# Loading x ahead of the small vectors, and giving the context rows a root of their own

## The reference, cut to what matters

```python
mods_x = jnp.split((silu_c @ w_mod[l] + b_mod[l])[:, None, :], N_MOD, axis=-1)    # 2048 -> 6 * 2048
mods_c = jnp.split((silu_cc @ w_mod[l] + b_mod[l])[:, None, :], N_MOD, axis=-1)
nc = modulated_norm(h_c, attn_norm[l], mods_c[0], mods_c[1])   # rmsnorm(x) * g * (1 + scale) + shift
pc = nc @ w_in[l][:, Q_END:KR_END]                             # context: keys and values only
nx = modulated_norm(h_x, attn_norm[l], sa_x, sca_x)
... = jnp.split(nx @ w_in[l], ...)                             # latent: q, kv, rotary key, short convolution
o_mla = mla_attention(...)                                     # 8 heads, latent queries, latent + context keys
h_new = h_x + ga_x * merge_head_groups(o_mla, o_conv, p)
h_new = h_new + gf_x * moe_ffn(modulated_norm(...), p)         # router, 32 experts (top 4), shared expert
return rmsnorm(h_x, final_norm)
```

## Time and profile before

| | |
|---|---|
| median of 3 runs | 1144.02 us (1142.94 to 1144.53) |
| the profiled execution's own time | 1142.15 us |
| its span, first to last instruction | 1140.3 us |
| PE busy | 1024.8 us (90%) |
| DVE busy | 551.8 us (48%) |
| ACT busy | 223.3 us (20%) |
| loads and stores | 380.30 MB, mean 334 GB/s |
| chain that ended last | PE 70%, DMA 12%, DVE 8%, SP's queue 4%, ACT 4% |

### The profile page before, as it was taken

How to read it: one execution, slowest core, us unless ns; L and a number is a source line. 1 busy time by engine, 2 the same in 40 slices (tenths; PEclk the granted TensorE clock), 3 DMA queues, 4 the chain that set the end, 5 groups by cost and what they waited for, 6 DMA issues and landing times.

```text
span 1140.3 us, 15754 instructions
## 1 busy us (share of the span) xinstructions
PE 1024.8 (90%) x6029; PEld 575.9 (51%) x6041; DVE 551.8 (48%) x1104; ACT 223.3 (20%) x449; POOL 8.7 (1%) x13
## 2 busy tenths in 40 slices
PE   0899999999999998999989998987979988998985
PEld 0544578888875355444476753333334334333431
DVE  1300186854814783885465053454255354455433
ACT  4311110000002354010142022122022122123112
POOL 0000000000000000000000000000000000000002
PEclk9899999999999999999999999999989999999998
DMA  8989979999845736999709989999999999999994
GB/s 333 390 325 389 381 233 361 371 346 324 276 160 185 257 111 220 330 387 344 253 22 354 389 332 370 409 409 408 407 409 408 407 406 408 409 407 409 409 404 188
DMA packets 158359, 380.30 MB, mean 334 GB/s; under 512 B 10498, under 2 KB 44112, under 8 KB 157136
## 3 DMA queue, kind: packets, MB, share of 16 engines
q1 hardware_dynamic: 158288, 379.35, 88.9%
HBM read 377.22 MB, written 2.10 MB: 333 GB/s over the span
## 4 chain that ended last, share of the span: by engine, by line
PE 70%; DMA 12%; DVE 8%; SPq 4%; ACT 4%; issue 2%; POOL 0%; ACTq 0%; DVEq 0%
PE ps L623 68%; DMA ring<-in_w_exp_down 8%; SPq L523 4%; DVE xres L1917 3%; DMA ring<-in_w_mod 1%; DMA qnT<-in_w_mod 1%; DVE nreg L1874 1%; DMA ring<-in_ctx 1%; ACT nreg L1157 1%; PE ps L692 1%; DVE nreg L1911 1%; DVE part L1907 1%; DVE tiny L1647 0%; ACT ring L1311 0%; PE ps L871 0%
## 5 line engine op out<-in xcount | busy, mean ns | idle before, releaser
L623 PE MATMUL ps<-nreg,ring 128*128 128x256 f32 (+2 forms) x1312 | 308.5, 400 | 8.3 <-ACT nreg L1157 5.9
L623 PEld LDWEIGHTS ps<-nreg,ring 128*128 128x128 f32 (+1 forms) x1312 | 245.4, 191 | 65.8 <-issue 23.9
L1500 DVE SCALAR_TENSOR_TENSOR part<-ring,csT,part 128x512 f32<-128x512 f32 x232 | 174.4, 752 | 8.9
L623 PE MATMUL ps<-ring,nreg 128*32 128x512 f32 (+1 forms) x1344 | 171.1, 599 | 7.0 <-DMA ring<-in_w_exp_up 7.0
L623 PE MATMUL ps<-ring,conv 128*32 128x512 f32 (+2 forms) x688 | 99.8, 631 | 20.7 <-DMA ring<-in_w_exp_down 19.8
L623 PE MATMUL ps<-ring 128*128 128x512 f32 x256 | 110.8, 592 | 0.0
L623 PEld LDWEIGHTS ps<-ring,nreg 128*32 128x32 f32 (+1 forms) x1344 | 50.4, 114 | 117.7 <-issue 117.7
L623 PE MATMUL ps<-nreg,conv 128*128 128x512 bf16 x231 | 58.8, 378 | 27.4 <-DVE xres L1917 26.8
L623 PEld LDWEIGHTS ps<-ring 128*128 128x128 f32 x256 | 48.6, 190 | 60.4 <-issue 60.3
L1917 DVE TENSOR_TENSOR xres<-xres,ps 128x512 f32<-128x512 f32 x96 | 61.5, 682 | 25.2 <-PE ps L623 25.2
L623 PEld LDWEIGHTS ps<-ring,conv 128*32 128x32 f32 (+2 forms) x688 | 29.0, 120 | 82.9 <-issue 79.2
(11 more groups left out here) (231 smaller groups left out, 935.4 us busy)
## 6 DMA issues: line engine op xcount, KB each, us to landing
ring<-in_w_mod SPq DMA_DIRECT2D x78, 1024.0 KB, 10.6
ring<-in_w_exp_gate SPq DMA_DIRECT2D x128, 512.0 KB, 13.9
ring<-in_w_exp_up SPq DMA_DIRECT2D x128, 512.0 KB, 15.3
ring<-in_w_exp_down SPq DMA_DIRECT2D x128, 512.0 KB, 14.1
ring<-in_w_in SPq DMA_DIRECT2D x12, 2048.0 KB, 13.5
ring<-in_w_out SPq DMA_DIRECT2D x8, 2048.0 KB, 10.3
ring<-in_w_mod SPq DMA_DIRECT2D x3, 2048.0 KB, 19.7
ring<-in_w_in SPq DMA_DIRECT2D x3, 1664.0 KB, 15.9
```

Of the source, the lines that this page charges most:

```text
L623: return nc.tensor.matmul(o, l, r, start=start, stop=stop)
L1500: ins = V.scalar_tensor_tensor(out=out_, in0=w_, scalar=scale, in1=acc_, op0=ALU.mult, op1=ALU.add)
```

## The change

1. SP issues `x` first, then `cst` with a semaphore of its own (`cst_in`), then the ten other small loads, then `ctx`. GpSimd's first root and PE's first transpose wait for `cst_in`.
2. The one root over four columns becomes two: columns 8 and 9 (x) as soon as x has been squared, columns 10 and 11 (ctx) later. Later waits on `root` count one more.
3. Each pair of tiles is now scaled by both engines: tile 0 by DVE, tile 1 by ACT, for x and then for ctx. The squares of ctx go to `kq` as bfloat16, since `nreg` by then holds transposed x.
4. ACT does the squares of x and its half of the scaling before the SiLU; `small_in` counts to 10 loads.
5. PE transposes all of x (`rows_T`, 8 steps of 4 transposes, two column blocks in one bank), then does half of the first modulation group, then all of ctx, then the other half. One eviction now takes 128 x 512: eight on DVE for x, eight on ACT for ctx, in place of sixteen of 128 x 256 on each.

```diff
+            sp.dma_start(xres[:, :, :], x[0].rearrange("(t p) d -> p t d", p=P)).then_inc(x_in, 16)
+            sp.dma_start(cst[:, :], consts[:, 0:NCONST]).then_inc(cst_in, 16)
             sp.dma_start(crow[0:KC, :], c.rearrange("b (c p) -> (b c) p", p=P)).then_inc(small_in, 16)
...
-            sp.dma_start(cst[:, :], consts[:, 0:NCONST]).then_inc(small_in, 16)
...
-            sp.dma_start(xres[:, :, :], x[0].rearrange("(t p) d -> p t d", p=P)).then_inc(x_in, 16)
...
-            power(tiny[:, 8:12])
+            pool.wait_ge(cst_in, 16)
+            power(tiny[:, 8:10])
+            power(tiny[:, 10:12])
...
+            def rows_T(rows, done, side):
+
+                for j in range(KC // 2):
+                    if j >= 3:
+                        pe.wait_ge(done, j - 2)
+                    for k in (2 * j, 2 * j + 1):
+                        for t in range(2):
+                            at = T * (k % 2) + 128 * t
+                            ins = nc.tensor.transpose(ps[:, 2 * (j % 3) + side, at:at + 128], rows[:, t, 128 * k:128 * k + 128],
+                                                      ident)
+                    ins.then_inc(xT_full, 1)
+
             pe.wait_ge(xs_ready, 2)
+            rows_T(xs, xT_lat, 0)
+            pe.wait_ge(small_done, 1)
+            for k in range(8):
+                first_rows(0, k)
             pe.wait_ge(ctxs_ready, 2)
...
+            rows_T(ctxs, xT_ctx, 1)
+            for k in range(8, KC):
+                first_rows(0, k)
...
-            sc.wait_ge(small_in, 16 * 11)
-            nc.scalar.activation(csil[:, :], crow[0:32, :], ACT.Silu).then_inc(silu_c, 1)
...
+            sc.wait_ge(root, 1)
+            nc.scalar.activation(xs[:, 1, :], xres[:, 1, :], ACT.Identity, scale=tiny[:, 9:10]).then_inc(xs_ready, 1)
+            sc.wait_ge(small_in, 16 * 10)
+            nc.scalar.activation(csil[:, :], crow[0:32, :], ACT.Silu).then_inc(silu_c, 1)
             sc.wait_ge(ctx_ld, 16)
+            squared = kq[:, :].bitcast(BF16)
...
+            for j in range(KC // 2):
+                sc.wait_ge(xT_full, KC // 2 + j + 1)
+                copy(nT[:, 2 * j:2 * j + 2, T:2 * T], ps[:, 2 * (j % 3) + 1, :].rearrange("p (k t) -> p k t", k=2))\
+                    .then_inc(xT_ctx, 1)
...
+            ve.wait_ge(squares, 2)
+            rsqrt(tiny[:, 8:10], stat[:, 0:2], D)
+            V.tensor_scalar(xs[:, 0, :], xres[:, 0, :], tiny[:, 8:9], None, ALU.mult).then_inc(xs_ready, 1)
...
+            for j in range(KC // 2):
+                ve.wait_ge(xT_full, j + 1)
+                V.tensor_copy(nT[:, 2 * j:2 * j + 2, 0:T], ps[:, 2 * (j % 3), :].rearrange("p (k t) -> p k t", k=2))\
+                    .then_inc(xT_lat, 1)
             ve.wait_ge(squares, 4)
-            rsqrt(tiny[:, 8:12], stat[:, 0:4], D)
...
+            rsqrt(tiny[:, 10:12], stat[:, 2:4], D)
+            V.tensor_scalar(ctxs[:, 0, :], ctxs[:, 0, :], tiny[:, 10:11], None, ALU.mult).then_inc(ctxs_ready, 1)
```

More of the change, by code:

```diff
@@ L255, in block_kernel @@
         m_used = sem("m_used")
+        cst_in = sem("cst_in")
         zeroed, silu_c, small_T, small_done = sem("zeroed"), sem("silu_c"), sem("small_T"), sem("small_done")
@@ L623, in mm @@
                 return nc.tensor.matmul(o, l, r, start=start, stop=stop)
+            pe.wait_ge(cst_in, 16)
             pe.wait_ge(silu_c, 1)
@@ L629, in _ @@
             nc.tensor.transpose(ps[:, 7, 256:352], brow[0:96, :], ident[0:96, 0:96]).then_inc(small_T, 1)
-            pe.wait_ge(small_done, 1)
             def mod_cols_of(n, b, bank=5):
@@ L701, in _ @@
             mod_cols_of(1, 1, 7)
-            pe.wait_ge(xT_lat, KC)
-            pe.wait_ge(xT_ctx, KC)
+            pe.wait_ge(xT_lat, KC // 2)
+            pe.wait_ge(xT_ctx, KC // 2)
             def query_set(s, ms):
@@ L1166, in _ @@
                                      accum_out=stat[:, t:t + 1]).then_inc(squares, 1)
+            sc.wait_ge(root, 1)
+            nc.scalar.activation(xs[:, 1, :], xres[:, 1, :], ACT.Identity, scale=tiny[:, 9:10]).then_inc(xs_ready, 1)
+            sc.wait_ge(small_in, 16 * 10)
+            nc.scalar.activation(csil[:, :], crow[0:32, :], ACT.Silu).then_inc(silu_c, 1)
             sc.wait_ge(ctx_ld, 16)
+            squared = kq[:, :].bitcast(BF16)
             for t in range(2):
-                nc.scalar.activation(nreg[:, 2048 * t + 4096:2048 * t + 6144], ctxs[:, t, :], ACT.Square,
+                nc.scalar.activation(squared[:, 2048 * t:2048 * t + 2048], ctxs[:, t, :], ACT.Square,
                                      accum_out=stat[:, t + 2:t + 3]).then_inc(squares, 1)
@@ L1177, in rows_out @@
                 copy(part[:, b, :], ps[:, bank, :]).then_inc(part_full, 1)
[L1180 to L1187, removed]
+            sc.wait_ge(root, 2)
+            nc.scalar.activation(ctxs[:, 1, :], ctxs[:, 1, :], ACT.Identity, scale=tiny[:, 11:12]).then_inc(ctxs_ready, 1)
+            for j in range(KC // 2):
+                sc.wait_ge(xT_full, KC // 2 + j + 1)
+                copy(nT[:, 2 * j:2 * j + 2, T:2 * T], ps[:, 2 * (j % 3) + 1, :].rearrange("p (k t) -> p k t", k=2))\
+                    .then_inc(xT_ctx, 1)
             rows_out(0, 7, 0, True)
             rows_out(1, 7, 1, True)
-            sc.wait_ge(xT_ctx, KC)
+            sc.wait_ge(xT_ctx, KC // 2)
             for s in range(SETS):
@@ L1305, in _ @@
                                          ACT.Square, accum_out=hsum[:, t, n:n + 1]).then_inc(hsq, 1)
-            sc.wait_ge(root, 2)
+            sc.wait_ge(root, 3)
             sc.wait_ge(mods_ready, 1)
@@ L1424, in _ @@
                         sc.wait_ge(over_sq, 4 * t + n + 1)
-            sc.wait_ge(root, 3)
+            sc.wait_ge(root, 4)
             for n in range(4):
@@ L1515, in gate_out @@
                 V.tensor_tensor(chunk, chunk, ps[:, 5, :], ALU.add).then_inc(modT_done, 1)
+            for j in range(KC // 2):
+                ve.wait_ge(xT_full, j + 1)
+                V.tensor_copy(nT[:, 2 * j:2 * j + 2, 0:T], ps[:, 2 * (j % 3), :].rearrange("p (k t) -> p k t", k=2))\
+                    .then_inc(xT_lat, 1)
             ve.wait_ge(squares, 4)
-            rsqrt(tiny[:, 8:12], stat[:, 0:4], D)
[L1520 to L1525, removed]
+            rsqrt(tiny[:, 10:12], stat[:, 2:4], D)
+            V.tensor_scalar(ctxs[:, 0, :], ctxs[:, 0, :], tiny[:, 10:11], None, ALU.mult).then_inc(ctxs_ready, 1)
             cols_out(0, MOD_ORDER[0], 7)
             cols_out(1, MOD_ORDER[1], 7)
-            ve.wait_ge(xT_lat, KC)
+            ve.wait_ge(xT_lat, KC // 2)
             for s in range(SETS):
```

## The result

| | before | changed |
|---|---|---|
| median of the runs shown with the result | 1144.28 us (4 runs) | 1135.75 us (4 runs, 1134.4 to 1135.99) |
| ratio, 95% interval | | 0.9941 (0.9919 to 0.9962) |
| second comparison, another chip | 1141.78 us (28 runs) | 1136.96 us (11 runs), ratio 0.9959 (0.9939 to 0.9979) |
| third comparison | 1142.45 us (26 runs) | 1137.62 us (9 runs), ratio 0.9964 (0.9949 to 0.9979) |
| the profiled execution, span | 1142.15 us, 1140.3 us | 1135.97 us, 1134.2 us |

Four executions in a slow state (three of before, one of experiment 2, 1247 us and more) are left out of the medians.

A forecast was written before the change was run, and what follows sets the result against it. Load stream and PE's list, tied by a hole in the loads, bound the start; the stream could gain 1.8 + 4.9 = 6.7 us but gains PE's 6.5, so median 1144.02 becomes 1137.5 us. Range 1135.3 to 1141.5.

The forecast's parts named there:

- Two chains, tied by the hole: Up to 112 us the load stream and PE's list run side by side; only time both gain reaches the end.
- Which of the two is the smaller: By the hole near 60 us the stream could gain 6.7 us, PE's list 6.5, so PE decides.
- By busy share ... 1.8 us are won.: Load stream, 2 to 8 us: with x in front the queue has work from the start, moving later landings 1.8 us.
- The landing of x, the two roots, the table load.: Start: x lands at 8.2 us, first root 4.99, second table load 1.28, SiLU to 16.8, PE on x at 17.65.
- I count 24 transposes at 0.228.: PE's transposes of x: 24 at half speed take 5.5 us, to 23.1; all 32 end at 24.6.
- With the 1.8 that is 37.5, before it is needed.: The second modulation group's last piece lands at 37.5 us, so PE does not wait for it.
- The wait for all 16 steps of `xT_full`: SP's wait before the second quarter of group 2 ends at 32.7 us and no longer holds anything.
- The clock rival: PE's clock falls at 28.3 us in a 1.8 us gap; PE gains 3.7, a 3.0 us hole remains, 1140.3 us; chance 0.25.
- 4.9 us long: Hole in the loads from about 61.8 to 66.7 us, while SP stands in `wait_used`; it closes but for 0.2.

The follow-up runs named there:

- experiment 2: Kernel before with the new load order alone (x first, constants on their own semaphore), compute order as before; 1140.93 against 1141.78 us, ratio 0.9999.
- Experiment 8: Changed kernel with a one-element SiLU first (one table) and identity transposes filling PE's gaps; 1138.74 us, ratio 0.9963.
- Experiment 6: Changed kernel with one added activation of 128 x 4096 (3.6 us) on ACT ahead of its tile of ctx; 1138.12 us, ratio 0.9969.
- Experiment 10: Changed kernel with one more unused load of 1 MiB behind the first quarter of group 3; 1139.88 us, ratio 0.9981, against the changed kernel's 1137.62.
- experiment 7: Kernel before with 28 identity transposes in PE's gaps between 41 and 50 us; 1140.82 against 1142.31 us, ratio 0.9993.
- experiment 9: Kernel before with one more unused load of 1 MiB behind the first quarter of group 3; 1143.24 against 1142.45 us, ratio 1.0005.
- experiment 3: Changed kernel with the old load order (small loads, then x, then ctx); 1139.57 against 1141.78 us of before, ratio 0.9978.
- experiment 4: Changed kernel with a one-element SiLU as ACT's first operation, so the second table load goes; 1136.22 us, ratio 0.9958.
- experiment 5: Changed kernel with one added activation of 128 x 2048 (some 1.9 us) on ACT ahead of its tile of ctx; 1136.74 us, ratio 0.9958.

## Why the prediction was right, and what in it was not

**Two chains, tied by the hole.** Right. The stream and PE's list each gained, and the smaller gain counted. Experiment 8 moved PE's list 2.5 us forward where SP goes on, with nothing to show for it at the last group. Experiment 6 moved it 3.05 back, and 2.0 of them came through as a hole. Experiment 10 moved the stream, and the last group went with it.

**Which of the two is the smaller.** Not as forecast. PE was to gain 6.5 us and to leave 0.2 of the hole. It gained 6.1 up to the projection (44.32 against 43.9 forecast) and 1.3 more inside it, since the spell there was 3.4 us long and not 6.8: 7.3 where SP goes on. The hole closed fully and the stream gave what it had, 1.4 + 4.9 = 6.3. That this is so near 6.5, and the trace's 1135.97 us so near the 1135.7 forecast for it, is in part luck. So is the tail behind the last group, which differed by only 0.2 us between the two traces.

**"By busy share ... 1.8 us are won."** The stream gained 1.4 (ctx 1.45 earlier in experiment 2).

**The landing of x, the two roots, the table load.** x was squared from 8.54 and not 8.2, and the steps behind it kept that lateness of 0.3: the SiLU ended at 17.14 (16.83 + 0.31) and not 16.8. PE's first transpose of x came 0.2 late. The trace has the table load at 1.28 us with nothing around it (15.52 to 16.83), so the 2.66 us of the Trainium skill ("ScalarE: Activation LUTs", "What ACT_TABLE_LOAD costs") is not seen here.

**"I count 24 transposes at 0.228."** Mis-sized: all 32 took 5.66 us and not 6.9, and between 5.4 and 6.4 us in the other traces of the changed list, as the slow start ends at another point in each. PE began on ctx at 27.52 and not 28.5.

**"With the 1.8 that is 37.5, before it is needed."** Wrong, without effect: `hb` landed at 39.4, as late as before, and PE waited 0.22 us for it. I do not know why the loads that landed near 39 us gained nothing, while those up to 35 us had gained 1.3. The wait for all 16 steps of `xT_full` also did not vanish as forecast; it held SP until 32.9, without effect on the flow (389 GB/s).

**The clock rival.** Half right. The clock fell at 28.4 where the rival had 28.3, and it fell again at 45.5. But the spell lasted 3.4 us and not the 6.8 of the earlier trace rows, so the transposes of ctx took 5.38 us where the rival had 7.0. The price I gave was the length of one spell in one trace. In thirteen traces the sum of half-clock time between 24 and 62 us was anything from 0 to 10.2 us, for the same PE list too (3.4 and 6.8 in the changed kernel). In experiments 7 and 8, with the gaps filled, there was no spell; in experiments 2 and 9 there was none with the gaps open. So a gap of 2.5 us alone did not decide it here, and what did is open. The Trainium skill's page "TensorE: Matmul & The Clock Gate", section "Part 1: The HAM clock gate", says that an idling engine is put to half its clock. The traces agree only in part: behind the same gap ahead of the projection the clock fell in the first trace of before and stayed at 1.00 in experiment 2's.

**The step that was mis-sized is the hole.** The text took "4.9 us long" from one trace and made it the gain of every execution. Of those 4.9 us some 3 belong to the spell behind 49.5 us, as experiment 7 shows (hole 1.8 without it). An execution of before like experiment 7's has 1.8 to win there, and 1.4 + 1.8 = 3.2 in all; one like experiment 9's some 0.8 and 2.2; one like the first trace has 6.3. The two larger comparisons, 4.8 us each, lie between. The term of 1.8 us for the stream measured 1.4. The forecast of 6.5 stood at the upper end of what the mechanism can give, and the first comparison's 8.5 us, from four runs on each side, is not reached by it at all (its interval, 0.9919 to 0.9962, goes down to 4.3 us). So the time of 1135.75 lies within the range by runs that came out low and not by the mechanism. That the spread of the tail (below) explains the rest is likely, but it is not shown for those four runs.

## What to carry to other kernels

Where a queue of loads runs beside an engine's list and both are near full, look for the hole in the loads and ask who opens it: moving the engine's list forward pays until the hole is closed, and no further (experiment 8). An extra load ahead of the place tests for a hole, since it costs less where there is one; but set its trace against an execution with the same PE timing, or the price comes out wrong. And do not take the length of a hole, or of a spell at half clock, from one trace; a second trace of the same kernel is worth more than a finer reading of the first.

## What the runs showed that I had not expected

The part of the program behind the last group is the same in all these kernels, yet it took between 1027.8 us (before, the changed kernel, experiments 2, 3, 4) and 1033.6 us (experiment 5) in thirteen traces. The start is not where they part. In eleven of them the reciprocal near 410 us stands within 0.03 us of 304.27 behind the wait; in the second trace of the changed kernel and in experiment 5 it stands 1.7 us later, and both have a spell at half clock near 390 us (clock 0.79 from 386 to 394 us) that the first trace does not have (1.00). The rest arises further on. The changed kernel first, then experiment 5, one stretch of the expert passes each:

```profile
684.00:1104.00 420.00, 371.30 (x2998) 159.25 (x2991) 191.81 (x413) 90.05 (x192) 0.00 (x0) 0.98 1.03 407
```

```profile
684.00:1104.00 420.00, 371.65 (x2989) 158.19 (x2985) 191.22 (x412) 89.14 (x190) 0.00 (x0) 0.97 1.03 406
```

One hundredth of the mean clock over 420 us is 4.2 us of full-clock time, or 8.4 us spent at half clock. But the clock does not explain all of it. Experiments 9 and 10 also have 0.97 in this stretch, and their tails are among the short ones (1028.3 us each), while experiment 8 has 0.98 and 1033.3. What else lengthens a tail is open. So an execution's time is a poor witness for a change of 5 us at the start (experiment 5's profiled execution took 1141.55 us with a start as good as the changed kernel's), and the position of one wait in the trace is a good one: 106.15, 105.75, 105.91 for the changed kernel.
